# Banded attention: stationary values in two column halves, and the division ahead of the turn

## The reference

```python
def sink_softmax(s, sink):
    sk = sink.astype(jnp.float32)[:, :, None, None]
    m = jnp.maximum(jnp.max(s, axis=-1, keepdims=True), sk)
    e = jnp.exp(s - m)
    return e / (jnp.sum(e, axis=-1, keepdims=True) + jnp.exp(sk - m))
...
        p = sink_softmax(jnp.concatenate([s_band, s_ctx], axis=-1), sink_g)
        vv = jnp.concatenate([vb, vc], axis=1)
        return jnp.einsum('bkgqj,bjkd->bqkgd', p.astype(v.dtype), vv)
```

## Time and profile before

| | |
|---|---|
| median of 3 runs | 1774.96 us (1773.62 to 1777.56) |
| profiled execution, span | 1773.1 us, mean granted TensorE clock 0.998 |
| TensorE busy | 1735.4 us, 98% of the span |
| VectorE, ScalarE, GpSimd busy | 1222.1, 803.9, 767.4 us |
| banded attention | from 714.5 us (first scores) to about 905 us |

### The profile page before, as it was taken

How to read it: one execution, slowest core, us unless ns; L and a number is a source line. 1 busy time by engine, 2 the same in 40 slices (tenths; PEclk the granted TensorE clock), 3 DMA queues, 4 the chain that set the end, 5 groups by cost and what they waited for, 6 DMA issues and landing times. The chain is left out here.

```text
span 1773.1 us, 25768 instructions
## 1 busy us (share of the span) xinstructions
PE 1735.4 (98%) x9180; PEld 1478.7 (83%) x9180; DVE 1222.1 (69%) x1720; ACT 803.9 (45%) x1577; POOL 767.4 (43%) x494
## 2 busy tenths in 40 slices
PE   8999999999998999999999999899999999999998
PEld 6997888888887999899988878778888888888887
DVE  3628688879948999688833366875666566575767
ACT  3435333435637888656510145633333333344453
POOL 1407577767533898520022232465555555400000
PEclk9999999999999999999999999999999999999999
DMA  8233233435767665412034242233223323385734
GB/s 349 86 109 137 96 119 155 164 133 190 262 181 199 170 146 146 142 33 72 1 143 160 90 166 87 80 109 117 95 98 126 119 95 128 115 281 201 257 105 178
DMA packets 98567, 249.86 MB, mean 141 GB/s; under 512 B 12321, under 2 KB 26017, under 8 KB 98338
## 3 DMA queue, kind: packets, MB, share of 16 engines
q1 hardware_dynamic: 98466, 248.52, 41.9%
HBM read 183.07 MB, written 65.41 MB: 140 GB/s over the span
## 5 line engine op out<-in xcount | busy, mean ns | idle before, releaser
L750 POOL TENSOR_TENSOR ring<-raw_w,ring 128x512 fp32r<-128x512 f32 x120 | 186.8, 1574 | 138.4 <-ACT ring L621 138.3
L78 PE MATMUL psum<-h_hi,ring 128*128 128x512 f32 x400 | 155.8, 390 | 3.0 <-ACT z L667 2.0
L80 PE MATMUL psum<-h_hi,ring 128*128 128x512 f32 x400 | 155.6, 389 | 0.0
L79 PE MATMUL psum<-h_lo,ring 128*128 128x512 f32 x400 | 155.6, 389 | 0.0
L78 PE MATMUL psum<-u_slot 128*128 128x512 f32 x308 | 120.4, 391 | 1.0 <-DVE u_slot L2953 0.8
L80 PE MATMUL psum<-u_slot 128*128 128x512 f32 x308 | 120.2, 390 | 0.0
L79 PE MATMUL psum<-u_slot 128*128 128x512 f32 x308 | 119.9, 389 | 0.0
L621 ACT ACTIVATE ring<-raw_w 128x512 fp32r<-128x512 f32 x120 | 72.5, 626 | 100.5 <-DVE raw_w L915 32.0
L1406 DVE TENSOR_REDUCE mx<-psum 128x1 f32<-128x1280 f32 x64 | 95.1, 1486 | 9.2 <-PE psum L1292 8.8
L1339 ACT ACTIVATE e<-psum,neg_m 128x1280 f32<-128x1280 f32 x64 | 85.0, 1328 | 31.2 <-DVE neg_m L1407 31.2
L2552 POOL TENSOR_TENSOR cut_lo<-i_raw,cut_hi 128x512 fp32r<-128x512 f32 x44 | 66.8, 1519 | 59.3 <-ACT cut_hi L2407 59.3
(11 more groups left out here) (413 smaller groups left out, 5219.9 us busy)
## 6 DMA issues: line engine op xcount, KB each, us to landing
raw_w<-in_w_pairs SPq DMA_DIRECT2D x40, 512.0 KB, 4.5
qk_dram<-room SPq DMA_DIRECT2D x26, 512.0 KB, 3.6
room<-in_w_ada SPq DMA_DIRECT2D x24, 512.0 KB, 5.3
gates_dram<-ost SPq DMA_DIRECT2D x24, 512.0 KB, 3.0
b_g<-gates_dram SPq DMA_DIRECT2D x8, 1536.0 KB, 7.6
stage<-in_w_ff SPq DMA_DIRECT2D x22, 512.0 KB, 5.9
i_raw<-in_w_ff SPq DMA_DIRECT2D x22, 512.0 KB, 4.9
f_dram<-h SPq DMA_DIRECT2D x22, 512.0 KB, 3.3
```

Source lines behind the costliest of these rows:

```text
L78: pe.matmul(out, sh, mh, start=first, stop=False, skip_group_check=onto)
L79: pe.matmul(out, sh, ml, start=False, stop=False, skip_group_check=onto)
L80: return pe.matmul(out, sl, mh, start=False, stop=last, skip_group_check=onto)
L750: pool.tensor_tensor(w_lo[i], source(p, i), w_hi[i].bitcast(F32), ALU.subtract).then_inc(w_lo_ready, 1)
```

## The change

- The products swap their operands. The values (128 keys x 64) are stationary, the turned square (128 keys x 128 queries) moves, and the two heads write partitions 0 to 63 and 64 to 127 of the same 128 columns, alternating head by head for each key tile. The result is already turned: `out`, `output` and `o` are gone, and `output_hi` and `output_lo` read the products' bank in step i-2.
- The division therefore moves ahead of the turn: `normalise` multiplies each head's `e` (128x512 or 128x640) in place by its reciprocal; VectorE does so for units 0 to 8, GpSimd for units 9 to 31, together with `sinks`. `turn` now waits for it.
- `pt` is used as a row of squares, so that each part is one copy; ScalarE copies parts 0 and 2, VectorE part 1, and VectorE's copy stands ahead of `reciprocals(i)`. `output_lo(i-2)` is last.
- GpSimd's multiplications `on` are spread over its new loop.
- The merge's first products are placed otherwise, ScalarE's high parts of their weights come a step earlier and in another place.

```diff
-        o = [sb(f"wo{b}", [P, 2, HD]) for b in range(2)]
+        sb("wgap", [P, 4, HD])
...
+        def weights_at(u):
+
+            return pt[u % 2][:].rearrange("p s k n -> p (s k) n")
+
+        def group(u, part):
+
+            return weights_at(u)[:, 4 * part:4 * part + len(squares(u)[part]), :]
+
         STEPS = UN + 3
+        LAST = UN - 1
+        POOL_FROM = 9
...
-            if 0 <= i - 3 < UN:
-                ring["out", i - 3, 0] = len(ring)
...
             def turn(u):
-                for s in range(2):
-                    pe.wait_ge(exp_done[s], u + 2)
                 for part, todo in enumerate(squares(u)):
                     b, bank = use("turn", u, part)
+                    for s in sorted({s for s, _ in todo}):
+                        pe.wait_ge(norm_ready[s], u + 1)
...
-                b, bank = use("av", u)
-                tiles = tiles_of(u)
-                for s in range(2):
-                    for n, k in enumerate(tiles):
-                        mm = pe.matmul(bank[:, s * HD:(s + 1) * HD], pt[u % 2][:, s, n, :], val[kv][:, k, :], start=(n == 0),
-                                       stop=(n == len(tiles) - 1))
+                b, _ = use("av", u)
+                tiles, out = tiles_of(u), out_of(u)
+                for n, k in enumerate(tiles):
+                    for s in range(2):
+                        mm = pe.matmul(out[s * HD:(s + 1) * HD, :], val[kv][:, k, :], weights_at(u)[:, s * len(tiles) + n, :],
+                                       start=(n == 0), stop=(n == len(tiles) - 1))
                 mm.then_inc(turned[b], 1)
...
                 if i == UN + 1:
+                    first["product"](pe, 0, range(2, BC))
+                if 0 <= i - 2 < UN:
+                    products(i - 2)
+                if i == UN:
                     for s in range(2):
                         pe.wait_ge(exp_done[s], UN + 1)
                     pe.wait_ge(*final("da", GROUPS - 1))
-                    first["product"](pe, 0)
-                if i == UN + 2:
-                    pe.wait_ge(*final("pool", GROUPS - 1))
-                    first["product"](pe, 1, range(2))
-                if 0 <= i - 2 < UN:
-                    products(i - 2)
+                    first["product"](pe, 0, range(2))
                 if 0 <= i - 1 < UN:
                     turn(i - 1)
-                if 0 <= i - 3 < UN:
-                    out(i - 3)
...
-            first["product"](pe, 1, range(2, BC))
+            pe.wait_ge(*final("pool", GROUPS - 1))
+            first["product"](pe, 1)
...
                 if i < UN:
                     sinks(i)
-                if 0 <= i - 3 < UN:
-                    output_hi(i - 3)
+                if 0 <= i - 2 < UN:
+                    output_hi(i - 2)
+                if 0 <= i - 1 < UN:
+                    copy_out(i - 1, 0)
+                    copy_out(i - 1, 2)
...
+        def normalise(eng, u, s):
+            row = e[u % 2][s][:, 0:len(tiles_of(u)) * P]
+            eng.wait_ge(rec_ready, u + 1)
+            eng.tensor_scalar(row, row, rec[:, u % 4, s:s + 1], None, ALU.mult).then_inc(norm_ready[s], 1)
...
+            normed(0)
+            normed(1)
+            for u in range(POOL_FROM, UN):
+                sinks(pool, u)
+                for s in range(2):
+                    normalise(pool, u, s)
+                g, rest = divmod(u - 4, 3)
+                if rest == 0 and 2 <= g < GROUPS:
+                    normed(g)
+                if u == UN - 2:
+                    first["pool"](pool, 0)
+            first["pool"](pool, 1)
+            first["pool"](pool, 2)
...
+            def output_lo(u):
...
-                v.tensor_tensor(y_lo[2][here], banks[4 + b][:, 0:P], y_hi[2][here].bitcast(F32), ALU.subtract).then_inc(free[b], 1)
+                v.tensor_tensor(y_lo[2][here], out_of(u), y_hi[2][here].bitcast(F32), ALU.subtract)\
+                 .then_inc(free[slot("av", u)[0]], 1)
...
                 if i < UN:
                     maximum(ch, i, 0)
                     maximum(ch, i, 1)
-                    sinks(i)
+                    if i < POOL_FROM:
+                        sinks(v, i)
...
+                if 0 <= i - 1 < UN:
+                    copy_out(i - 1, 1)
+                if i < UN:
+                    reciprocals(ch, i)
+                if i < POOL_FROM:
+                    for s in range(2):
+                        normalise(v, i, s)
                 if 0 <= i - 2 < UN:
-                    output(i - 2)
-                if 0 <= i - 1 < UN:
-                    for part in range(1, len(squares(i - 1))):
-                        copy_out(i - 1, part)
+                    output_lo(i - 2)
...
-                if 0 <= i - 3 < UN:
-                    output_lo(i - 3)
-                if i < UN:
-                    reciprocals(ch, i)
```

More of the change, by code:

```diff
@@ L1549, in final, with out_of @@
             return free[b], used + 2
-        keep["branches"] = {"rows": final("out", UN - 1), "ring": [last_use(b) for b in range(4)]}
+        def out_of(u):
+            return banks[4 + slot("av", u)[0]][:, 0:P]
+        keep["branches"] = {"rows": final("av", LAST), "ring": [last_use(b) for b in range(4)]}
         def y_part(part, branch, g):
@@ L1748, in sinks, with copy_out @@
                 act.activation(es[:, u % 2, :], es[:, u % 2, :], ACT.Exp).then_inc(es_ready, 1)
-            def copy_out(u):
-                b, used = slot("turn", u, 0)
+            def copy_out(u, part):
+                if part >= len(squares(u)):
+                    return
+                b, used = slot("turn", u, part)
                 act.wait_ge(turned[b], used + 1)
-                act.activation(pt[u % 2][:, 0, 0:4, :], banks[4 + b].rearrange("p (k n) -> p k n", n=P), ACT.Copy)\
+                out = group(u, part)
+                act.activation(out, banks[4 + b][:, 0:len(squares(u)[part]) * P].rearrange("p (k n) -> p k n", n=P), ACT.Copy)\
                    .then_inc(free[b], 1)
@@ L1757, in output_hi @@
                 kv, blk, pair = at(u)
-                b, used = slot("out", u)
+                b, used = slot("av", u)
                 act.wait_ge(turned[b], used + 1)
-                act.activation(y_hi[2][:, kv * 2 + pair, blk * P:(blk + 1) * P], banks[4 + b][:, 0:P], ACT.Copy).then_inc(yc_hi_ready, 1)
+                act.activation(y_hi[2][:, kv * 2 + pair, blk * P:(blk + 1) * P], out_of(u), ACT.Copy).then_inc(yc_hi_ready, 1)
             def row_copy(n):
@@ L1838, in _, with normed @@
             pool.wait_ge(rms_ready, 1)
-            for g in range(GROUPS):
+            def normed(g):
                 if g >= 2:
@@ L1843, in _ @@
                                         ss[:, 4 * g:4 * g + 4].unsqueeze(2).to_broadcast([P, 4, P]), ALU.mult).then_inc(on_ready, 1)
-            for n in range(3):
-                first["pool"](pool, n)
+            normed(0)
[11 more added lines that the diff above has]
+            first["pool"](pool, 2)
         @block.vector
@@ L1856, in maximum @@
                  .then_inc(neg_ready[s], 1)
-            def sinks(u):
-                kv, blk, pair = at(u)
-                head = kv * WA_GROUP + 2 * pair
-                for s in range(2):
-                    v.wait_ge(neg_ready[s], u + 1)
-                v.tensor_tensor(es[:, u % 2, :], neg_m[:, u % 2, :], sink[:, head:head + 2], ALU.add).then_inc(es_in_ready, 1)
             def reciprocals(ch, u):
@@ L1869, in reciprocals, with copy_out @@
                 ch.link(v.tensor_tensor(sums[:, u % 2, :], sums[:, u % 2, :], es[:, u % 2, :], ALU.add))
-                ch.link(v.reciprocal(rec[:, u % 4, :], sums[:, u % 2, :]))
-            def output(u):
-                b, used = slot("av", u)
+                v.reciprocal(rec[:, u % 4, :], sums[:, u % 2, :]).then_inc(rec_ready, 1)
+            def copy_out(u, part):
+                b, used = slot("turn", u, part)
                 v.wait_ge(turned[b], used + 1)
+                v.tensor_copy(group(u, part), banks[4 + b].rearrange("p (k n) -> p k n", n=P)).then_inc(free[b], 1)
+            def output_lo(u):
+                kv, blk, pair = at(u)
                 if u == 0:
```

46 lines of the change are left out of this document (12 added, 34 removed).

## The result

| | before | after |
|---|---|---|
| median of 4 runs each | 1774.8 us (1773.62 to 1777.56) | 1796.34 us (1795.39 to 1798.17) |
| ratio | | 1.0122 (1.0107 to 1.0136) |
| span of the profiled execution | 1773.1 us | 1795.1 us |
| TensorE, VectorE, ScalarE, GpSimd busy | 1735.4, 1222.1, 803.9, 767.4 us | 1721.8, 1210.5, 809.4, 856.0 us |

The change makes the kernel 21.5 us slower. TensorE has 14 us less to do and waits 36 us more. The forecast was 6.5 us slower, 1781.5.

A forecast was written before the change was run, and what follows sets the result against it. TensorE's order was taken to set the pace. Triples +0.5, steps 14 to 18 -1.7, early divisions and waits +9.5, tail -1.8: +6.5 us on 1774.96, so 1781.5, range 1769 to 1799.

The forecast's parts named there:

- GpSimd's division: From unit 9: 1.0 us per 128x640 division, between 0.76 and 1.3, covered before the turn's second part; at 1.3 all but 0.1.
- the new wait: Pool products, da turns and row sums wait for VectorE's low output part to free their ring slot; TensorE idles 1.3 to 1.5 us.
- products block: A unit's 20 product matmuls, halves overlapping, with two stationary-width changes: 1.4 us, about 0.8 less than before.
- Rival A: The two product halves don't run at once, block 2.2 + 0.3 us; some +15 more, 1797 us; chance 0.17.
- rival D: GpSimd's division is the bound, at 1.3 us and stretched by VectorE: 1784 us; counted inside the forecast's 0.43 chance.
- Plain steps: Steps with neither pool product nor da turn: VectorE's work sets 4.2 us, TensorE's is 4.0; 4.70 before.
- da step: Step with a da turn: the turn waits for VectorE's low output part, 5.35 + 0.38 = 5.75 us; 5.53 before.
- The early steps: Steps 2 to 8: VectorE's divisions, waits in steps 4, 5, 7 and sums held by GpSimd, 47.1 against 39.28; +9.5 up to step 9.
- the divisions on VectorE wait for GpSimd: Units 0 to 8: the SBUF port shared with GpSimd can hold the divisions too, adding up to 2 us more.
- B: Faster: block about 1.1 us, sums not held by GpSimd, early divisions 0.4 apiece, no width-change cost; 1770.5 us, chance 0.25.
- C: No change, within 3.5 us: early loss of 4 to 6, the rest as forecast; 1776 us, chance 0.15.
- The prediction's own test: In the profile, pool products that start without a wait would make the whole prediction wrong, to the fast side.

The follow-up runs named there:

- run 2: The changed kernel, with GpSimd's division from unit 9 made a two-input product with the reciprocal broadcast instead of a tensor_scalar: 1781.68 us.
- run 1: The changed kernel, with both output copies earlier: ScalarE's high part between the exponentials, VectorE's low part ahead of its copy and reciprocals: 1783.5 us.
- run 4: The changed kernel, with all products of head 0 issued, then all of head 1, instead of alternating: 1805.17 us, two executions.
- run 7: The changed kernel, with the division from unit 9 on left out but for one column: 1778.02 us.
- run 5: The changed kernel with two repairs together, the early output copies of run 1 and the two-input GpSimd division of run 2: 1756.35 us.
- run 10: The kernel of run 5, with the products issued one head after the other instead of alternating: 1767.02 us.
- run 11: The kernel of run 5, with VectorE's reciprocals and early division ahead of its copy of the turned part in all units: 1753.71 us.
- run 12: The kernel of run 5, with VectorE's reciprocals ahead of its copy of the turned part from unit 9 on only: 1754.73 us.
- run 3: The changed kernel, with VectorE's sum, reciprocals and early divisions ahead of its copy of the turned part: 1792.97 us.
- run 6: The changed kernel, with VectorE's division in units 0 to 8 left out but for one column: 1790.16 us.
- run 8: The kernel of run 5, with ScalarE dividing head 1 in units 0 to 8, which VectorE did: 1761.29 us.
- run 9: The kernel of run 8, with GpSimd dividing from unit 7 on instead of unit 9: 1757.88 us.

## Why the prediction was right, and where its size was wrong

| | forecast | measured |
|---|---|---|
| up to step 9 | +9.5 | +13.1 |
| steps 9 to 30 | -1.2 | +11.2 |
| tail | -1.8 | -2.2 |
| whole | +6.5 | +22.1 (spans), +21.5 (medians) |

**The direction and the main mechanism were right.** About half of the loss, though, lies in steps 9 to 30 and has a cause that the sum put at nothing, GpSimd's division. Either cause alone would have made the kernel slower: run 2, with a division inside the forecast's range, is at 1781.68, run 1, with the new wait all but gone, at 1783.5. The new wait stands where it was put: pool step 5.96 (forecast 6.15), ahead of pool products 0.96, ahead of da turns 1.11, none in steps 15, 16 and 18, and behind the low part in each case. The products block was forecast at 1.4 and measured 1.24, plus 0.1 between scores and products (0.21 instead of the 0.12 from one score to the next). Rival A falls; run 4 shows its mechanism in a kernel that doesn't alternate, with a block of 1.95 where it had 2.5.

**The step that failed is the price of GpSimd's division.** "I take 1.0", between 0.76 and 1.3 of the earlier trace rows. Measured 1.89. Both ends were rows of other operations: a cast with one input and a product with two. The upper one seemed safe, since a second tensor seemed the dearest thing an operation could have. Run 2 shows that the two-input product of this width takes 1.25, inside the range; only the form with a scalar operand is dearer than both. The Trainium skill (GPSIMD Engine Reference, section Engine selection) calls one-input operations on GpSimd roughly line-rate; by this trace the one-input form takes 3.4 times VectorE's 0.55, and the measurement decides. At 1.89 the division is no longer covered: the second part of the turn, "that needs both", would start at 7.5, against a reciprocal at 4.85 and two of 1.89, 8.6, so a wait of 1.1. The turn waits 13.0 us in all, and a division of 1.25 (run 2) gives back 13.9 us of steps 9 to 30, one of a single column (0.28, run 7) 17.2. Of rival D, which had the right engine, only the mechanism was right: its price stopped at 1.3.

With a division inside the range, the sum holds: run 2 has 1781.68, the forecast was 1781.5. Part of that is luck, since it is 2.7 us faster than before in steps 9 to 30 (forecast 1.2) and 12 slower early. Plain steps were forecast at 4.2 and take 3.85: VectorE is not the bound in them. The da step, forecast at 5.75, takes 7.30, but 5.63 with the division left out (run 7).

**The early steps** were forecast at 47.1 us and take 51.3. Of the seven step lengths (4.8, 6.05, 7.9, 9.3, 6.4, 7.4, 5.2), steps 4, 5 and 7 are far off, with 11.45, 10.65 and 9.54. The three steps with the new wait were counted with one wait each, behind the same step's work of VectorE. But the square-root table's loads on ScalarE reached VectorE only in step 4, so that its maxima began at 745.26, when the turn was about to start, and the whole of its step then lay between the turn and the row sums. A second term was left out altogether, the clock:

```profile
L1693 PE MATMUL psum<-late_rows,early 128*128 128x512 f32 x8 | 7.3, 1064 | 6.5 <-DVE y_lo L1912 6.5
```

The eight matmuls of the row sums had a mean of 615 ns before and in runs 1, 5, 10, 11 and 12, where no wait ahead of them was over 1.64. In the others it is higher: 1064 after waits of 3.22 and 3.23, 1046 after 3.22 and 3.21 (run 7), 923 after 3.22 and 2.80 (run 2), 843 after 3.22 and 3.34 (run 3), 1036 after 2.55 and 2.53 (run 4), 716 after 3.21 and 2.37 (run 6), and after a single one of 2.35 803 (run 8) and 628 (run 9). So a longer wait does not always cost more. In all of these others but run 9 the granted clock of the stretch is 0.87 to 0.96 of 2.4 GHz, so part of it ran at 1.2, and the row sums and the scores behind them pay. (Runs 5, 11 and 12 have 0.96 too, but there it fell later, in steps 7 and 8.) How much of the early loss is the clock alone was not measured apart. An estimate is possible from run 1, whose TensorE does the same work in steps 2 to 8, at 1.00:

```profile
731.71:770.68 38.97, 32.76 (x284) 26.18 (x283) 34.87 (x84) 24.59 (x63) 15.62 (x12) 1.00 0.49 129
```

TensorE is busy 32.76 us there and 38.75 after the change, and idle 6.2 and 12.6: of the 12.35 us between the two, about half is the lower clock and half the waits themselves.

The prediction also let the divisions on VectorE wait for GpSimd, for up to 2 us. In step 0 they do: the two of unit 0 take 2.60 us, from 722.45, beside GpSimd's product of 128x1024 from 722.69 to 724.77, and the two of unit 1, with GpSimd idle, 0.88. From step 2 on no product of GpSimd ran beside them, two took 1.02, and the term came to nothing.

**Rivals.** B (faster) asked for a block of 1.1 and sums that aren't held. It got most of the first, and neither the held sums nor the waits let it through; but run 5 shows that its side was open: what the two repairs gave back was 40 us. (Its terms, -3.2, -1.4, -4.8 and -0.9, add up to a change of -3.8 and 1771.2, not to -4.5 and 1770.5.) C falls.

**The prediction's own test** ("pool products that start without a wait would make the whole prediction wrong") is what run 1 came to from step 10 on: there they start without one, and that kernel was not faster either, since the wait for GpSimd had taken the place. The sentence took one wait for the only one.

## What to carry to other kernels

When an operand leaves a shared ring of buffers, work out anew for every later user which instruction frees its slot, and put that instruction as early in its engine's order as its data allow; here two moved calls were worth 12.8 us, and more once the next wait was gone. Repairs of waits in one loop need not add: price them together (12.8 and 14.7 us alone, 40.0 together), and don't drop one because alone it changed little. An operation that moves to another engine needs a price from the same form on that engine, and where there is none, the upper bound should reach beyond the nearest forms.

## What the runs showed of the hardware that had not been expected

- GpSimd multiplies a 128x640 float32 tile by a scalar per partition in 1.89 us, and by the same scalar as a broadcast second tile in 1.25. With 512 columns it is 1.57 against 1.04. VectorE's form with the scalar takes 0.55.
- Float32 products with 64 stationary columns, alternated between the two halves of the output partitions, start every 0.055 us (20 in 1.31, of which the last takes 0.27); with one half after the other every 0.092 (20 in 2.02).
- VectorE's operations on two columns, 0.16 us alone, lasted up to 1.9 us while GpSimd worked on two operands of 1024 columns; in run 8, where VectorE reached them earlier, they still ended with GpSimd's operation.
- VectorE's multiplication of a 128x512 tile by a scalar per partition, with that tile as its only wide operand, was held by GpSimd's two-input products as well: two of them took 2.60 us after the change and 3.12 in run 5 (from 722.68), against 0.88 with GpSimd idle. Beside GpSimd's one-input cast (771.62 to 772.56 after the change) two of 128x640 took their usual 1.02.
